# RWKV-7 block on one core: the chunks of the recurrence issued two units at a time on four quarters of the matmul array

## The reference, cut to what matters

```python
def step(state, inp):
    r_t, w_t, k_t, v_t, kk_t, a_t = inp
    sa = jnp.einsum('bhij,bhj->bhi', state, kk_t)
    state = (state * w_t[:, :, None, :]
             + jnp.einsum('bhi,bhj->bhij', -sa, kk_t * a_t)
             + jnp.einsum('bhi,bhj->bhij', v_t, k_t))
    return state, jnp.einsum('bhij,bhj->bhi', state, r_t)
...
_, y = lax.scan(step, s0, xs)
mean = jnp.mean(y, axis=-1, keepdims=True)
var = jnp.mean(jnp.square(y - mean), axis=-1, keepdims=True)
y = ((y - mean) * lax.rsqrt(var + GN_EPS)).reshape(bsz, s, RWKV_WIDTH) * ln_g + ln_b
```

## Time and profile before

| | us |
|---|---|
| median of 3 runs | 1352.61 (1352.37 to 1354.55) |
| profiled execution, its own time | 1352.39 |
| its span, first to last instruction | 1350.6 |
| input projection | 0 to 267 |
| recurrence | 267 to 372.5 |
| output projection, norm, router | 372.5 to 418 |
| experts | 418 to the end |
| TensorE busy over the span | 93% |
| mean granted TensorE clock | 0.980 |

### The profile page before, as it was taken

One profiled execution on the slowest core, in us unless ns is written; L12 is line 12 of the kernel. 1 busy time (PEld: TensorE's weight loads), 2 busy tenths in 40 slices (PEclk: granted clock), 3 DMA queues, 4 the chain that ended last, 5 costly groups with the idle time before them and its releaser, 6 DMA issues.

```text
span 1350.6 us, 22390 instructions
## 1 busy us (share of the span) xinstructions
PE 1256.0 (93%) x9961; PEld 667.8 (49%) x9961; DVE 327.5 (24%) x557; ACT 215.2 (16%) x341; POOL 61.4 (5%) x34
## 2 busy tenths in 40 slices
PE   6999999999999999999899899989989989989996
PEld 5888888899954333433333333333333333333332
DVE  1114484145534111211111111111211111211112
ACT  4121131143212100100001110000110000110001
POOL 0000000065311000000000000000000000000000
PEclk9999999999998999999999999999999999999999
DMA  9333353211196999999999999999999999999993
GB/s 304 130 125 125 129 183 125 78 57 26 32 413 255 430 428 436 428 432 431 427 430 434 433 428 432 427 431 430 434 431 433 428 428 429 437 427 432 432 429 143
DMA packets 43007, 449.74 MB, mean 333 GB/s; under 512 B 5264, under 2 KB 6544, under 8 KB 26480
## 3 DMA queue, kind: packets, MB, share of 16 engines
q1 hardware_dynamic: 39680, 445.58, 78.7%
q10 hardware_dynamic: 3280, 3.43, 0.9%
HBM read 447.95 MB, written 1.05 MB: 332 GB/s over the span
## 4 chain that ended last, share of the span: by engine, by line
PE 66%; DMA 30%; DVE 2%; ACT 1%; issue 1%; ACTq 0%; SPq 0%; DVEq 0%
DMA ring<-in_exp_w 30%; PE ps L701 20%; PE ps L407 17%; PE ps L736 10%; PE ps L474 5%; PE ps L667 3%; PE ps L658 2%; PE ps L590 2%; PE ps L476 1%; PE ps L490 1%; PE ps L714 1%; PE ps L691 1%; DVE work L1307 1%; PE ps L723 1%; PE ps L439 1%
## 5 line engine op out<-in xcount | busy, mean ns | idle before, releaser
L701 PE MATMUL ps<-ring,work 128*64 128x512 f32 x2048 | 471.4, 616 | 48.3 <-DMA ring<-in_exp_w 48.3
L701 PEld LDWEIGHTS ps<-ring,work 128*64 128x64 f32 x2048 | 150.9, 141 | 351.6 <-issue 276.2
L407 PE MATMUL ps<-work,ring 128*128 128x256 f32 (+1 forms) x1120 | 235.0, 380 | 0.6 <-ACT work L767 0.6
L736 PE MATMUL ps<-ring,work 128*64 128x512 f32 x1024 | 225.1, 592 | 0.0
L407 PEld LDWEIGHTS ps<-work,ring 128*128 128x128 f32 (+1 forms) x1120 | 201.6, 185 | 33.7 <-issue 5.0
L1296 DVE TENSOR_SCALAR work<-ps 128x512 f32<-128x512 f32 x32 | 22.1, 692 | 500.5 <-PE ps L701 500.5
L935 ACT ACTIVATE work<-work 128x512 f32<-128x512 f32 x32 | 20.1, 630 | 734.7 <-DVE work L1296 734.7
L736 PEld LDWEIGHTS ps<-ring,work 128*64 128x64 f32 x1024 | 72.4, 136 | 129.6 <-issue 129.6
L1312 DVE COPY work<-ps 128x512 f32<-128x512 f32 x32 | 22.1, 692 | 208.2 <-PE ps L736 208.2
L667 PE MATMUL ps<-work 64*128 64x512 f32 x264 | 65.6, 615 | 0.8 <-DVE work L1312 0.8
L658 PEld LDWEIGHTS ps<-sel,work 128*128 128x128 bf16 x1536 | 53.7, 118 | 24.3 <-issue 24.3
(11 more groups left out here) (228 smaller groups left out, 785.1 us busy)
## 6 DMA issues: line engine op xcount, KB each, us to landing
ring<-in_exp_w SPq DMA_DIRECT2D x64, 4096.0 KB, 29.2
ring<-in_exp_w SPq DMA_DIRECT2D x64, 2048.0 KB, 30.1
ring<-in_w_in SPq DMA_DIRECT2D x16, 2048.0 KB, 7.7
ring<-in_w_out SPq DMA_DIRECT2D x2, 2048.0 KB, 8.6
ring<-in_w_in SPq DMA_DIRECT2D x1, 1152.0 KB, 8.6
work<-in_x SPq DMA_DIRECT2D x2, 512.0 KB, 4.1
work<-in_x ACTq DMA_DIRECT2D x2, 512.0 KB, 4.1
out<-work SPq DMA_DIRECT2D x2, 512.0 KB, 2.7
```

Of the source, the lines that this page charges most:

```text
L407: last = mm(ps[b % 4][width * g:width * g + width, 0:T], chunk(n)[:, k, c0:c0 + width], XN[:, k, :], start=k == 0, stop=k == KT - 1)
L701: last = mm(ps[4 + part][64 * half:64 * half + 64, :], xe[:, k * CAP:(k + 1) * CAP], ring[:, slot(u, k), part * D + half * 512:part * D + ...
L736: last = mm(ps[7][64 * half:64 * half + 64, :], lhs, ring[:, slot(u, 8 + j), i * D + half * 512:i * D + half * 512 + 512], start=False, st ...
```

## The change

- All four chunks are in flight in one list of 70 calls of `go`, which issues one unit or two at a time, interleaved product by product. In a pair, one unit uses the two quarters of the array on the diagonal and the other the two off it. For that the factors, transposes and some merges (`MERGE_AT`) write head `q` to the partitions of the other head (`swap`), and later units read them there.
- Transposes are products with the identity, in one bank of 128 partitions, evicted by ScalarE in one instruction. That for V multiplies by `centre64` (identity less 1/64), so that Y comes out centred, and VectorE's `centre` is gone.
- The state's old value is added on the array (`s_keep`, a product with the identity into the open bank), so `advance` is one instruction. `below64` is gone: ScalarE copies the bank to mL unmasked (its `lower`), which the pair masks of the corners make enough.
- Z, Y and S are opened with their values' part ahead of the state's part. The serial pass for chunks 0 and 1 runs beside the merges of chunks 2 and 3; `turn_y(2)` moves ahead of the output projection, whose second product (0, 1) is now in one piece.
- `first_e` takes single chunks and stands between POOL's large products, and writes mE. The b1 loads move from ScalarE's list to SP's, ahead of the experts'; ScalarE's wait for b1_split, the b2 and gffn loads stand between `take_u(1)` and `turn_e(3, 1)`.
- Two more temporaries in `ring[:, 4]` and `ring[:, 5]`; PSUM banks are assigned per chunk.

The diff, cut to its core:

```diff
-            def product(bank, lhs, rhs, opens=None, closes=None):
+            def go(*units):
                 for m in range(KT):
                     for q in range(2):
...
+                        for bank, a, b_, swap, opens, closes, done in units:
+                            o = ps[bank][rows(q ^ swap), cols(m)]
+                            if opens is None:
+                                last = mm(o, a(q, m), b_(q, m), start=True, stop=True)
+                            else:
+                                last = mm(o, a(q, m), b_(q, m), start=opens and m == 0, stop=closes, skip_group_check=True)
+                            if m == KT - 1 and q == 1:
+                                last.then_inc(done, 1)
+            def whole(bank, a, b_, swap, done):
+                return bank, a, b_, swap, None, None, done
-                        last = nc.tensor.transpose(ps[banks[q]][0:HEAD, cols(m)], src(q, m), C("ident64", 64)[rows(q)])
+            BANK_A, BANK_B = (4, 6, 0, 2), (5, 7, 1, 3)
+            Z, U, S_, Y_, TURN_Y = 4, 5, 6, (7, 7, 0, 7), (1, 2, 3, 2)
+            MERGE_AT = ((0, 1, 0), (1, 0, 1), (0, 0, 1), (1, 0, 0))
...
+                return whole(factor_bank(c, i), a, b_, 1, pe_f[c])
+            f_rb = lambda c: factor(c, 0, heads(AA, c), heads(R, c))
+            f_ak = lambda c: factor(c, 1, heads(Kt, c), heads(KK, c))
+            f_rk = lambda c: factor(c, 2, heads(Kt, c), heads(R, c))
+            turn_v = lambda c: factor(c, 3, heads(V, c), const("centre64"))
+            turn_b = lambda c: factor(c, 4, heads(AA, c), const("ident64"))
+            turn_k = lambda c: factor(c, 5, heads(Kt, c), const("ident64"))
...
+            def joined(c, lv):
+                pe.wait_ge(act_e[c], 3 + lv)
+                pe.wait_ge(dve_e[c], 6 + 2 * lv)
+                at = MERGE_AT[c][lv]
+                return whole(BANK_A[c], mat(mPT[c], at), mat(mP[c], at), 0, pe_e[c])
...
+            def s_keep(c):
+                pe.wait_ge(s_opened, c + 1)
+                pe.wait_ge(s_taken, c)
+                return S_, const("ident64"), state(c), 0, False, False, s_kept
...
+            go(upper(1), f_rb(0))
+            go(lower(1), f_ak(0))
+            go(upper(0), f_rb(1))
+            go(lower(0), f_rk(0))
+            go(turn_v(0))
+            go(square(1), f_ak(1))
...
+            go(joined(1, 0), series(2, 0))
+            go(joined(0, 0), f_rk(2))
+            go(square(3))
+            go(turn_e(1, 1), f_rb(3))
...
+            go(z_values(0), y_values(0))
+            go(s_values(0), joined(2, 0))
+            go(turn_b(3))
+            go(u_product(0))
+            go(z_values(1), turn_e(2, 1))
...
+            go(z_state(3), y_state(3))
+            go(y_u(2), turn_y(1))
+            go(u_product(3))
+            go(y_u(3))
+            go(turn_y(2))
...
-            turn_y(2)
-            out_product(0, 1, 0)
-            turn_y(3)
-            out_product(0, 1, 4).then_inc(wout_done, 1)
+            go(turn_y(3))
+            out_product(0, 1, 0, 8).then_inc(wout_done, 1)
# SyncE
+            sp.wait_ge(factors_ready, 5)
+            for s in range(3):
+                sp.dma_start(b1f[E * s:E * s + E, :], exp_b1[0]).then_inc(b1_in, 16)
# ScalarE: the transposed operands and E, in one instruction each
+            def turn_e(c, lv):
+                act.wait_ge(pe_e[c], 7 + 3 * lv)
+                af(mPT[c], ps[BANK_A[c]][:, :], ACT.Copy).then_inc(act_e[c], 1)
+            def lower(c):
+                act.wait_ge(dve_e[c], 2)
+                af(mL[c], ps[BANK_B[c]][:, :], ACT.Copy).then_inc(act_e[c], 1)
...
+            take_u(1)
+            act.wait_ge(b1_split, 7)
...
+            turn_e(3, 1)
+            take_z(2)
# VectorE
             def advance(c):
                 v.wait_ge(s_made, c + 1)
-                new, old = st[:, (c + 1) % 2], st[:, c % 2]
                 fade = dec[:, :, c:c + 1].to_broadcast([P, KT, HEAD])
-                got = by_m(ps[2][:, :])
-                if c:
-                    link(tt(new, old, got, ALU.add))
-                    got = new
-                tt(new, got, fade, ALU.mult).then_inc(s_taken, 1)
+                tt(st[:, (c + 1) % 2], by_m(ps[S_][:, :]), fade, ALU.mult).then_inc(s_taken, 1)
```

More of the change, by code:

```diff
@@ L173, in build @@
         y_made = sem("y_made")
-        y_taken = sem("y_taken")
         s_made = sem("s_made")
@@ L479, in turn @@
[L479 to L489, removed]
-                        last = nc.tensor.transpose(ps[banks[q]][0:HEAD, cols(m)], src(q, m), C("ident64", 64)[rows(q)])
-                return last
@@ new lines, in lower, with factor @@
+            def lower(c):
+                if c >= 2:
+                    pe.wait_ge(act_f[c - 2], 3)
+                return whole(BANK_B[c], heads(KK, c), heads(AA, c), 0, pe_e[c])
+            def factor(c, i, a, b_):
+                if c >= 2 and i == 0:
+                    pe.wait_ge(dve_e[c], 2)
+                    pe.wait_ge(act_e[c], 1)
+                elif c < 2 and i < 2:
+                    pe.wait_ge(blk_copied, LAST - (len(blocks) - 1 - factor_bank(c, i)) % 4)
+                else:
+                    before = i - 2 if c < 2 else i - 1
+                    if before < 3:
+                        pe.wait_ge(dve_f[c], before + 1)
+                    else:
+                        pe.wait_ge(act_f[c], before - 2)
+                return whole(factor_bank(c, i), a, b_, 1, pe_f[c])
@@ new lines, in _ @@
+            go(turn_b(0))
+            go(series(1, 0), turn_k(0))
+            go(series(0, 0), f_rk(1))
+            go(turn_v(1), upper(2))
+            go(series(1, 1))
+            go(series(0, 1), turn_b(1))
+            go(lower(2), turn_k(1))
+            go(series(1, 2))
+            go(series(0, 2))
+            go(f_rb(2), square(2))
+            go(turn_e(1, 0), upper(3))
+            go(corner(1, 0), turn_e(0, 0))
+            go(corner(0, 0), f_ak(2))
+            go(lower(3))
+            go(joined(1, 0), series(2, 0))
@@ new lines, in _ @@
+            go(joined(3, 0))
+            go(s_keep(1), turn_e(2, 2))
+            go(u_product(1), y_values(1))
+            go(corner(2, 2), turn_e(3, 1))
+            go(z_values(2), corner(3, 1))
+            go(s_u(1))
+            go(joined(2, 2))
+            go(y_state(1), joined(3, 1))
+            go(z_state(2), s_values(2))
+            go(y_u(1), turn_y(0))
+            go(s_keep(2))
+            go(u_product(2), turn_e(3, 2))
+            go(corner(3, 2), z_values(3))
+            go(y_values(2))
@@ L970, in _ @@
             pool.wait_ge(factors_ready, 5)
-            first_e(1)
             pool.wait_ge(b1_in, 48)
@@ new lines, in masked, with upper, lower, f_rb @@
+            def masked(dst, bank, name, made):
+                tt(by_m(dst), by_m(ps[bank][:, :]), mask(name), ALU.mult).then_inc(made, 1)
+            def upper(c):
+                v.wait_ge(pe_e[c], 1)
+                masked(mAT[c], BANK_A[c], "above8", dve_e[c])
+            def lower(c):
+                v.wait_ge(pe_e[c], 2)
+                masked(mA[c], BANK_B[c], "below8", dve_e[c])
+            def f_rb(c):
+                v.wait_ge(pe_f[c], 1)
+                masked(mRB[c], factor_bank(c, 0), "above_eq64", dve_f[c])
```

465 lines of the change are left out of this document (279 added, 186 removed).

## The result

The changed kernel took 1360.44 us (median of 5 runs, 1357.77 to 1361.67) against 1352.61 us for the kernel before in the same session (1352.10 to 1355.74): a ratio of 1.0047, 95% interval 1.0029 to 1.0064, so +3.9 to +8.7 us. The forecast was 1355.6 us within 1347 to 1364, slower with a chance of 0.5.

The account below looks back on a forecast made before the run. Instruction supply to TensorE was taken to bound the recurrence: first stop, 27 rounds, collisions and tail made the stage +4.3 us, less 1.1 behind it, net +3.2. 1352.39 + 3.2 gave 1355.6 us, range 1347 to 1364.

Parts of the forecast that it names:

- What binds: Recurrence: TensorE waits for instructions, one 256-instruction packet per 3.55 us round with one block in store; chance 82%.
- a pair of units in the 0.93 us of one: Recurrence, array: four quarters work at once, so a pair takes 0.93 us; 1.87 us if none overlaps.
- The first stop: Early recurrence: after 505 instructions TensorE stops for a packet behind w_out; ends near 275.2 us, between 274.3 and 275.9.
- The rounds: Recurrence after the first stop: 27 further instruction rounds of 3.55 us, 95.9 us in all.
- the collisions: Recurrence: b1 loads, and b2, gffn and x loads, each delay an instruction fetch by about 1 us; +2 us.
- the time from entering a block to its packet: Recurrence, each round: 1.0 us from TensorE entering a block until the next block's instruction packet starts.
- The tail: End of the recurrence: chain of the last three units (u, eviction, y, turn of y(2)) takes 3.7 us.
- Behind the stage: Output projection: the turn of y(2) is gone from between its halves, -1.1 us.
- That supply doesn't bind: Rival, recurrence: instruction supply sets no limit; stage 81 us, kernel about 1326 us; chance 10%.
- Two quarters at a time: Rival, recurrence: only two array quarters work at once; stage 119 us, kernel 1365 us; chance 5%.
- pairs at 1.6 us: Rival, recurrence: a pair takes 1.6 us; stage 107 us even with free supply, kernel 1353 us; chance 3%.
- the upper bound of 3.7: Recurrence: longest round allowed, 3.7 us, from the kernel before's fastest long stretch without a stop, 5 blocks in 18.7 us.

Follow-up runs that it names:

- run 3: Changed kernel with the two units of each call issued one after the other instead of interleaved product by product: 1360.44 us, ratio 1.0056 to the kernel before.
- run 8: Changed kernel with three 64-pass hardware loops ahead of the recurrence: one unit 0.93 us, pair on four quarters 1.10 us, pair on the same quarters 1.87 us.
- run 4: Changed kernel with the three small router loads issued some 100 us sooner, during the input projection: 1359.84 us, ratio 1.0056 to the kernel before.
- run 5: Changed kernel with 512 semaphore increments added on TensorE, eight in each of the recurrence's first 64 calls: 1418.59 us, ratio 1.0476 to the kernel before.
- run 1: Changed kernel with 512 TensorE no-ops added in the recurrence, which were not in the program the chip fetched: 1360.58 us, ratio 1.0055 to the kernel before.
- run 9: Changed kernel with half of each turn of mE, beta and k as transposes, a call's eight issued together ahead of its products: 1357.60 us, ratio 1.0041.

## Why the prediction was right, and what was off in it

**What binds** was read rightly. TensorE's 256-instruction rounds with one packet each, one block in store, stops inside units put down to nothing: these signs that the prediction named are in the trace, and the stage has 7567 instructions of TensorE where it counted 7580. Runs 3 and 8 show the mechanism from both sides. In loops, without fetches, a pair costs the 0.93 us of one unit; in the stage, paired and unpaired units take 113.8 and 114.0 us. The term "a pair of units in the 0.93 us of one" was right and worth nothing, as the prediction said.

**The first stop** ended 8.84 us after the stage's start against 8.2 forecast: +0.6. The forecast had it end 0.7 us sooner than before, as the block is used up faster. But its packet started 6.41 us after the stage's start, against 6.49 before: beside w_out and the router's loads nothing was gained (run 4: 1.3 us of the stop are the router's).

**The rounds** took 100.5 us against 95.9 + 2: +2.6. The two rounds in which the b1 loads (310.31 to 314.57) and the b2 and gffn loads (354.42 to 359.41) fell took 4.27 and 4.99 us, 2.2 us above 3.55; the collisions were well sized. The other 25 took 3.65 us instead of 3.55.

The mis-sized term is the time from entering a block to its packet. The forecast took 1.0 us for it, read off one single round, and 1.08 for the packet and 1.45 from there to work (3.53 in all, rounded up to 3.55). In the 20 rounds from 288.49 us on in which nothing else was on the DMA engines, the three parts took 1.28, 1.00 and 1.39 us on average, 3.67 in all. Half of these rounds took 3.44 to 3.56 us, the other half 3.65 to 4.10, and it is mostly the first part that differs: 1.05 to 1.75 us. Why the packet comes later in some blocks stays open. Increments put it back (run 5), so the waits in a block are a candidate, but some 30 waits more changed nothing measurable (run 1), and rounds with four of them took 3.55 us as well as 4.10.

**The tail** took 4.45 us (378.45 to 382.90) against 3.7: +0.75. The clock granted there was 0.51, the lower of its two levels, although the rounds ahead of it had the same kind of stops as earlier ones at 1.00; the last units ran at half speed, and y's last product waited 0.85 us for ScalarE.

The terms add up: 0.6 + 2.6 + 0.75 = 4.0, the difference between a stage longer by 8.2 us and the forecast +4.3. **Behind the stage** 2.4 us came back instead of 1.1. By the forecast 1.1 us are the moved turn of y(2); the rest wasn't followed.

**The rivals.** That supply doesn't bind is refuted by the stage's length and by run 3. Two quarters at a time, and pairs at 1.6 us, are refuted by run 8.

**In size** the forecast was short by half: +3.2 us, below the measured interval of +3.9 to +8.7. The range held the median, 1360.4 us. Two things that the prediction didn't consider moved the profiled execution: 2.1 us of its 8.0 came from when the input projection's first weights had landed, and behind the stage 1.3 us more came back than forecast, which by luck offset a third of what the stage was off. The round came out at 3.72 us over all 27, collisions included, just above the upper bound of 3.7 that the prediction had for a round without them.

No version beat the kernel before. The best try at fewer instructions (run 9) shortened the stage by 2 us, which its ratio doesn't show clear of noise; what stays open is a version of the changed order whose turns take half the instructions without changes of mode, or whose body is small enough to loop.

## What to carry to other kernels

Before packing more of the array with small matmuls, count instructions: with fp32 a product is four of them, and unrolled code was supplied here at 256 per 3.5 us, 55 ns a product, whatever the array could do. If the kernel is already near that (here 3.73 us used per block against 3.5 supplied), packing buys nothing. Increments that are instructions of their own lengthen it further: with some 17 in a block a round took 5.5 us instead of 3.7. A wait more per block didn't show. A small hardware loop is a quick way to see what the array would do without that limit, and the number of instruction packets tells whether an added instruction is in the program at all.

## What the runs showed of the hardware that was not expected

- In loops without fetches an increment of a semaphore cost TensorE 34 to 82 ns and a double wait long met 8 to 39 ns, the spread being what the loop's end adds; with some 17 increments in a block the next packet started 3.0 us after TensorE had entered it instead of 1.1 to 1.7 us.
- Transposes between tiled products cost 0.43 us for each transpose and product (0.64 us at the lower clock), 42 us in all, with a mean clock of 0.74 in the stage. Issued eight in a row they cost none of those 42 us, though TensorE was busy for 88 us instead of 77.
- 64 matmuls on four quarters of the array start 14.6 ns apart on average, at the price of 32.
- A stop of 4.9 us was followed by a granted clock of 0.51 for 6.9 us (276.9 to 283.8 us), and stops of 1.4 us in each 3.5 us left it at 1.00 except from 314.5 to 317.9 us, at the end of a stop of 2.3 us, and at the stage's end (0.51).
